# Where operand tiles begin inside 64 bytes: token tiles at a multiple of 64, weight tiles 32 bytes past one

## The chip, the cores and the metric

The kernel runs on one core of one Trainium2 chip. The metric is the device time of one execution in microseconds (us): the time before is 2825.68 us, the median of three runs from 2825.58 to 2825.96. A kernel's data lies in the core's on-chip memory (SBUF), 128 partitions wide; a tile's place is its first byte in every partition. TensorE multiplies: a stationary operand of up to 128 columns is loaded, and a moving operand of up to 512 columns streams past it.

## The reference, cut to what matters

Two blocks of two layers each work on 256 tokens of width 1024.

```
def reference(...):
    x = first_block(x, ...)      # 2 layers: x += mixers(rms(x) @ w_in) @ w_out
                                 #           x += peer_ffn(rms(x))
    return second_block(x, ...)  # 2 layers: x += merged(rms(x) @ w_in_2) @ w_o_2
                                 #           x += cross_attention(rms(x), rms(mem))
                                 #           x += (silu(h @ w1) * (h @ w3)) @ w2

def peer_ffn(x, w_query, sub_keys, down, up):   # 8 heads, top 16 of 16384 experts
    a = einsum('thkd,td->thk', down[ib], xb)
    c = gb * gelu(a)
    return einsum('thk,thkd->td', c, up[ib])
```

The kernel computes the expert layer densely: the activations of all 16384 experts (down), times a gate that is zero for the experts not chosen, times all of up. So nearly all work of both blocks is matrix products of a weight matrix with 256 tokens.

## The kernel before

**Three passes.** The products are float32. Every operand is split into a high part, rounded to the type fp32r, and a low part, what is left, and each product is made of three fp32r passes: high x high, and the two mixed ones. A weight chunk lands by DMA in `ring` (SyncE issues it some turns ahead), ScalarE copies it rounded into a high tile (`w_hi`, `out_hi`, `down_hi`, `up_hi` and others), and VectorE subtracts that from the raw one and writes the low tile (`ring_lo`, which lies over `ring`; `out_lo`, `down_lo`, `up_lo`). The token side has its own pairs: `h_t_hi` and `h_t_lo`, `h_t_expert` (the high part that goes with `h_t_lo` in the expert layer), `lead_x`, `held`, `coef`, `mt`, `ff`, `branch` and `ya`.

**Two shapes.** Where the result is wanted by channels, the weight tile is stationary (128 columns) and all 256 tokens are the moving operand: `channels` (L2648), `act_in_parts` (L1537), `passes_quarter` (L1480) and half of the front (L598). Where it is wanted by tokens, 128 tokens are stationary and 512 weight columns move: `tokens` (L2666), `branch` (L2925), `out_sums` (L1547), the held blocks (L1525) and the other half of the front (L607). In a row of the profile "ps<-a,b" is a product into PSUM with a moving and b stationary.

**Order.** Each engine has its list of instructions, written out by hand; semaphores order them across engines. TensorE runs one product after another, and the stationary operand of the next is loaded while the moving one of the present streams. In the peer loop 48 products of L1537 (one block of experts, 256 columns) alternate with 24 of L1547 (512 columns). The first 32 blocks of a layer's experts are held and summed by L1525 in one run of 768 products.

**Places.** Tiles are laid out one behind the other in the order of the code, `sb(...)` for those that stay; a `with ...: pass` gives its room back at once, so that the next tile lies over it. `arena` holds most of the rest, cut by `carve`, and tiles made by `over(...)` lie inside it. The first tile begins at byte 4224, a multiple of 64, and all sizes ahead of `hybrid_params` are multiples of 64 too. Its 69 numbers end 20 bytes past one; the next tile is put at the next multiple of 32. So before the change

- at a multiple of 64: `h_t`, `h_t_lo`, `ring` and `ring_lo`, `h_t_expert`;
- 32 bytes past one: everything behind, which is `out_hi`, `out_lo`, `coef`, `ya_hi`, `held`, `lead_x`, `first_hi`, `gate_hi`, `down`, `up`, `h_t_hi`, and in the second block `w_hi`, `mt`, `ff` and `branch`.

The pieces of these tiles that an instruction takes begin at multiples of 512 bytes within the tile, so that each operand has its tile's place inside 64 bytes.

Of the kernel before, what the change touches and what calls it, by code (L numbers as in the profile page):

```python
# [11 lines left out]
F32 = mybir.dt.float32  # L12
F32R = mybir.dt.float32r
# [4 lines left out]
P = 128  # L18
T = 256
D = 1024  # L20
TT = T // P
KD = D // P
# [22 lines left out]
GROUP = 8  # L45
# [5 lines left out]
STAGES = 4  # L51
GATES = T * NKEYS // 2
HELD = BLOCKS // 2
REACH = [(0, 0, 1, 16), (16, 1, 3, 8), (40, 4, 4, 4), (56, 8, 8, 1)]
REACHED = 64
PROB_BANKS = (4, 5, 6, 7, 2)
LEAD = HELD // 2 - 2
GATE_SPLIT = [LEAD, LEAD + 1]
# [4 lines left out]
for _n, _b in enumerate(LEAD_LOADS[4:]):  # L63
    LEAD_PLACE[_b] = LEAD_PLACE[_n]
LEAD_PLACE.update((b, ((0, 0), (1, 0), (0, 1))[b % 3]) for b in range(len(LEAD_LOADS), HELD))
LEAD_PLACE.update((b, (b % 2, 0)) for b in range(HELD, HELD + 2))
LOADS = LEAD_LOADS + list(range(len(LEAD_LOADS), HELD + 2))
LEAD_SLOTS = 5
FIRST_TURN = GATE_SPLIT[-1] + 1
OWN_X = FIRST_TURN + 2  # L70
TURNS = 2 * (HELD - FIRST_TURN)
TURN_HIGH = [next(s for s in range(GROUPS_OF_TOKENS) if QUARTER[s] >= 4 * (FIRST_TURN - LEAD) - 5 + 2 * n) for n in range(TURNS)]
# [25 lines left out]
HI_SLOTS, RAW_SLOTS, CHUNK_SIZE = 4, 8, 1024  # L98
# [80 lines left out]
N_SPAR = -(-N_SECOND // 16) * 16  # L179
N_Z3 = -(-2 * (T + 2) // 16) * 16  # L180
# [152 lines left out]
def build(nc, dram, out, steps):  # L333
    ctx = ExitStack()
    with ctx:
        def sb(name, shape, dt=F32):
            return ctx.enter_context(nc.sbuf_tensor(name, shape, dt))
# [9 lines left out]
        with nc.sbuf_tensor("h_t", [P, KD, T], F32) as HT:  # L347
            pass
        HT_LO = sb("h_t_lo", [P, KD, T], F32R)
        with nc.sbuf_tensor("ring_lo", [P, RAW_SLOTS, CHUNK_SIZE], F32R) as RAW_LO:  # L350
            pass
        RING = sb("ring", [P, 2, 4096])
        RAW = RING[:, :, :].rearrange("p a (b n) -> p (a b) n", n=CHUNK_SIZE)
        COMMON = sb("common_sb", [P, N_COMMON])
        with nc.sbuf_tensor("h_t_expert", [P, KD, T], F32R) as HT_EXPERT:
            pass
        PHASE = sb("phase_sb", [P, max(N_PHASE_CONST, KD * T)])
# [9 lines left out]
            pass  # L367

        with ExitStack() as second:
            second.enter_context(nc.sbuf_tensor("before_ya", [P, 3 * 512], F32))  # L370
            YA_HI = second.enter_context(nc.sbuf_tensor("ya_hi", [P, 2, T], F32R))
        GELU = sb("gelu", [P, 2, 512])
        COEF_HI, COEF_LO = sb("coef_hi", [P, 2, 512], F32R), sb("coef_lo", [P, 2, 512], F32R)
        KEYS = sb("keys", [P, P])
        with nc.sbuf_tensor("out_lo", [P, OUT_SLOTS, D], F32R) as OUT_LO:
            pass
        with nc.sbuf_tensor("hot_second1", [P, 2, GROUP, P], F16) as HOT2_ODD:
# [4 lines left out]
            pass  # L382
        sb("parts_room", [P, 4 * T])
        HOT2 = (HOT2_EVEN, HOT2_ODD)
        with nc.sbuf_tensor("arena", [P, 32768 + STAGES * GROUP * 64], F32) as ARENA:
            pass

        with ExitStack() as second:
            def over(name, shape, dt=F32R):
                return second.enter_context(nc.sbuf_tensor(name, shape, dt))  # L390

            BRANCH_LO = over("branch_lo", [P, KD, T])
            over("before_mem", [P, N_SPAR], F32)
            MT_HI, MT_LO = over("mt_hi", [P, KD, T]), over("mt_lo", [P, KD, T])
            over("before_w", [P, 2 * KD * T], F32)
            W_HI = over("w_hi", [P, HI_SLOTS, CHUNK_SIZE])
            FF_HI, FF_LO = over("ff_hi", [P, KF, T]), over("ff_lo", [P, KF, T])
            over("before_branch", [P, 4112], F32)
            BRANCH_HI = over("branch_hi", [P, 6, T])
        sb("arena_gates", [P, GATES])  # L400
        with nc.sbuf_tensor("held_lo", [P, HELD, 512], F32R) as HELD_LO:
            pass
        with nc.sbuf_tensor("before_gate_hi", [P, 17 * 512], F32), nc.sbuf_tensor("gate_hi0", [P, D], F32R) as GATE_HI0, \
                nc.sbuf_tensor("lead_x_hi", [P, KD, T], F32R) as LEAD_X_HI, nc.sbuf_tensor("lead_x_lo", [P, KD, T], F32R) as LEAD_X_LO, \
                nc.sbuf_tensor("first_hi", [P, 2, D], F32R) as FIRST_HI:
            pass
        DOWN_HI, DOWN_LO = sb("down_hi", [P, 2, 2 * D], F32R), sb("down_lo", [P, 2, 2 * D], F32R)
        UP_HI, UP_LO = sb("up_hi", [P, 2, 2 * D], F32R), sb("up_lo", [P, 2, 2 * D], F32R)
        with nc.sbuf_tensor("held_hi", [P, HELD_SLOTS, 512], F32R) as HELD_HI:
            pass  # L410
        with nc.sbuf_tensor("gate_hi1", [P, D], F32R) as GATE_HI1, nc.sbuf_tensor("gate_hi2", [P, D], F32R) as GATE_HI2:
            pass
        HT_HI = sb("h_t_hi", [P, KD, T], F32R)
        NUMBERS = sb("numbers", [P, P], F16)
# [68 lines left out]
        for n in (8, 8, 4, 2, 2):  # L483
# [9 lines left out]
        G = split(ARENA[:, 0:GATES], "p (t n) -> p t n", t=T)  # L493

        (SPAR, _, MT, MK, MV, _, Z3, YA, QKVG, ZG, GT, MER, QKR, QKT2, DM, MEMW), _ = carve(
            after_scr, N_SPAR, KD * T, KD * T, KD * T, TT * D, HI_SLOTS * CHUNK_SIZE, N_Z3, 2 * T, TT * 1536,
            TT * 512, TT * 3 * D, TT * D, TT * 512, 4 * T, 4 * (T + P), DEPTH * KD)
        FINAL = ARENA[:, after_scr + N_SPAR:after_scr + N_SPAR + D]
        WSM, VN, YC = (ONE[:, n * 512:(n + 1) * 512] for n in range(3))
# [208 lines left out]

        def late_stage(n):

            return 32768 + (n % STAGES if n >= STAGES else n - STAGES) * GROUP * 64

        def gates_of(n):

# [2728 lines left out]
```

## Time and profile before

| | |
|---|---|
| time of three runs, median | 2825.68 us |
| profiled execution: its own time | 2825.48 us |
| profiled execution: span of the core | 2823.7 us |
| granted TensorE clock, mean | 0.999 |
| TensorE matmuls busy | 2803.2 us, 99% of the span, 18566 of them |
| TensorE weight loads busy (beside them) | 2528.1 us, 90% |
| VectorE, ScalarE, GpSimd busy | 1943.8, 1419.7, 148.4 us |
| moved by DMA | 530.21 MB, 188 GB/s |

Busy is the time in which at least one instruction of the engine is under way. The span goes from the first instruction to the last; the execution's own time has 1.8 us around it. Matmuls overlap each other, so that the duration of one is longer than the time from its start to that of the next. "L2666" is line 2666 of the kernel.

### The profile page before, as it was taken

How to read it: one execution, taken by the hardware profiler on the slowest of the kernel's cores; microseconds unless marked ns; L12 is line 12 of the kernel's file. 1: busy time of each engine (PE TensorE's matmuls, PEld its weight loads, DVE VectorE, ACT ScalarE, POOL GpSimd, SP SyncE). 2: the span in 40 equal slices, each digit the busy share in tenths (PEclk: the TensorE clock that was granted, in tenths of full speed). 3: DMA queues.
4: the chain of work that ended last, by engine and by line, in shares of the span. 5: the costliest groups of instructions: out<-in, count | busy, mean ns of one | idle time of the engine just before them, and what ended most of it. 6: DMA issues, size and time to landing. Idle time of an engine off the chain costs nothing.

```text
span 2823.7 us, 45734 instructions
## 1 busy us (share of the span) xinstructions
PE 2803.2 (99%) x18566; PEld 2528.1 (90%) x18566; DVE 1943.8 (69%) x2882; ACT 1419.7 (50%) x1707; POOL 148.4 (5%) x145
## 2 busy tenths in 40 slices
PE   8999999999999999999999999999999999999998
PEld 7899998899999889999889999988899988888997
DVE  7889888655555788988865555576656556565664
ACT  6653554544444665355454444455455444545543
POOL 0033110000000003311000000000000000000000
PEclk9999999999999999999999999999999999999999
DMA  6344666855553534466685555465555656554663
GB/s 214 124 162 138 218 247 208 287 213 199 186 194 141 187 120 158 141 217 239 205 288 215 194 192 193 149 223 170 181 166 182 187 188 185 171 180 155 175 187 133
DMA packets 219570, 530.21 MB, mean 188 GB/s; under 512 B 13546, under 2 KB 87440, under 8 KB 208400
## 3 DMA queue, kind: packets, MB, share of 16 engines
q1 hardware_dynamic: 212944, 504.32, 54.2%
q0 software_dynamic: 6464, 23.61, 2.1%
q8 instruction: 116, 1.90, 0.3%
q14 instruction: 46, 0.38, 0.1%
HBM read 507.81 MB, written 20.06 MB: 187 GB/s over the span
## 4 chain that ended last, share of the span: by engine, by line
PE 98%; DVE 1%; DMA 1%; issue 0%; ACT 0%; SPq 0%; DVEq 0%
PE ps L2666 17%; PE ps L2648 13%; PE ps L1537 13%; PE ps L1547 12%; PE ps L1525 12%; PE ps L1480 11%; PE ps L607 4%; PE ps L598 4%; PE ps L1451 2%; PE ps L2925 2%; PE ps L1462 1%; PE ps L1255 1%; PE ps L2834 0%; PE ps L2818 0%; DMA ring<-in_peer_down 0%; PE ps L1367 0%
## 5 line engine op out<-in xcount | busy, mean ns | idle before, releaser
L2267 DVE TENSOR_TENSOR ring_lo<-ring,w_hi 128x1024 fp32r<-128x1024 f32 x320 | 388.2, 1224 | 243.0 <-ACT w_hi L2263 241.7
L2263 ACT ACTIVATE w_hi<-ring 128x1024 fp32r<-128x1024 f32 x320 | 335.2, 1056 | 236.1 <-PE ps L2666 169.0
L1537 PE MATMUL ps<-h_t_lo,down_hi 128*128 128x256 f32 x1024 | 288.2, 281 | 0.0
L1537 PE MATMUL ps<-h_t_expert,down_lo 128*128 128x256 f32 x1024 | 287.8, 281 | 0.0
L1537 PE MATMUL ps<-h_t_expert,down_hi 128*128 128x256 f32 x1024 | 286.8, 280 | 0.0
L2648 PE MATMUL ps<-h_t_lo,w_hi 128*128 128x256 f32 x928 | 260.7, 281 | 0.0
L2648 PE MATMUL ps<-h_t_hi,w_hi 128*128 128x256 f32 x928 | 259.4, 280 | 0.1
L2648 PE MATMUL ps<-h_t_hi,ring_lo 128*128 128x256 f32 x928 | 259.0, 279 | 0.0
L1143 ACT ACTIVATE out_hi<-ring 128x1024 fp32r<-128x1024 f32 x128 | 135.7, 1060 | 162.0 <-PE ps L1525 154.6
L2030 DVE TENSOR_TENSOR up_lo<-ring,up_hi 128x2048 fp32r<-128x2048 f32 x64 | 146.7, 2292 | 97.7 <-ACT up_hi L1134 97.7
L2023 DVE TENSOR_TENSOR out_lo<-ring,out_hi 128x1024 fp32r<-128x1024 f32 x128 | 156.6, 1224 | 77.1 <-ACT out_hi L1143 77.1
L1547 PE MATMUL ps<-up_hi,coef_hi 128*128 128x512 f32 x512 | 200.6, 392 | 0.0
L1547 PE MATMUL ps<-up_hi,coef_lo 128*128 128x512 f32 x512 | 199.9, 390 | 0.0
L1547 PE MATMUL ps<-up_lo,coef_hi 128*128 128x512 f32 x512 | 199.4, 390 | 0.0
L1525 PE MATMUL ps<-out_hi,held_hi 128*128 128x512 f32 x512 | 199.4, 389 | 0.0
L1525 PE MATMUL ps<-out_hi,held_lo 128*128 128x512 f32 x512 | 199.2, 389 | 0.0
L1525 PE MATMUL ps<-out_lo,held_hi 128*128 128x512 f32 x512 | 199.2, 389 | 0.0
L1134 ACT ACTIVATE up_hi<-ring 128x2048 fp32r<-128x2048 f32 x64 | 122.7, 1917 | 150.5 <-PE ps L1547 147.2
L1537 PEld LDWEIGHTS ps<-h_t_lo,down_hi 128*128 128x128 f32 x1024 | 193.0, 188 | 2.4
L1537 PEld LDWEIGHTS ps<-h_t_expert,down_hi 128*128 128x128 f32 x1024 | 192.5, 188 | 2.4
L1537 PEld LDWEIGHTS ps<-h_t_expert,down_lo 128*128 128x128 f32 x1024 | 193.3, 189 | 0.0
L2666 PE MATMUL ps<-w_hi,h_t_hi 128*128 128x512 f32 x448 | 180.3, 403 | 0.4 <-DVE ring_lo L2267 0.4
(532 smaller groups left out, 7403.5 us busy)
## 6 DMA issues: line engine op xcount, KB each, us to landing
ring<-in_peer_down SPq DMA_DIRECT2D x128, 1024.0 KB, 5.6
ring<-in_w_in SPq DMA_DIRECT2D x140, 512.0 KB, 3.7
ring<-in_peer_up SPq DMA_DIRECT2D x66, 1024.0 KB, 4.8
ring<-in_w SPq DMA_DIRECT2D x132, 512.0 KB, 3.8
ring<-in_peer_up SPq DMA_DIRECT2D x124, 512.0 KB, 4.2
late_gates<-arena POOLq DMA_DIRECT2D x64, 256.0 KB, 5.2
arena<-late_gates SPq DMA_DIRECT2D x16, 1024.0 KB, 6.4
ring<-in_w_out SPq DMA_DIRECT2D x16, 512.0 KB, 4.1
```

The source lines that it names most:

```text
L1134: a.e.activation(to[:, slot, :], raw(which, slot), ACT.Copy).then_inc(*a.count(name))
L1143: a.e.activation(OUT_HI[:, out_slot(b, j), :], up_raw(b, j), ACT.Copy).then_inc(*a.count(f"up_hi{b}{j}"))
L1480: m = pe.e.matmul(PS[:, act_bank(b), j * T:(j + 1) * T], w[:, o], x[:, kc, :], start=kc == 0 and n == 0, stop=kc == KD - 1 and n == 2)
L1525: m = pe.e.matmul(PS[:, 2 * t + half, :], x, w, start=b == 0 and j == 0 and n == 0, stop=False, skip_group_check=True)
L1537: m = pe.e.matmul(PS[:, 4 + b, j * T:(j + 1) * T], w[:, b, o], x[:, kc, :], start=kc == 0 and n == 0, stop=kc == KD - 1 and n == 2)
L1547: m = pe.e.matmul(PS[:, 2 * t + half, :], x[:, b, c], w[:, b, o], start=False, stop=last and n == 2, skip_group_check=True)
L2023: v.e.tensor_tensor(OUT_LO[:, out_slot(b, j), :], up_raw(b, j), OUT_HI[:, out_slot(b, j), :].bitcast(F32), ALU.subtract) \
L2030: v.e.tensor_tensor(lo[:, slot, :], raw(which, slot), hi[:, slot, :].bitcast(F32), ALU.subtract) \
L2263: a.e.activation(W_HI[:, g % HI_SLOTS, :], RAW[:, g % RAW_SLOTS, :], ACT.Copy).then_inc(*a.count(f"c{g}_hi"))
L2267: v.e.tensor_tensor(RAW_LO[:, g % RAW_SLOTS, :], RAW[:, g % RAW_SLOTS, :], W_HI[:, g % HI_SLOTS, :].bitcast(F32), ALU.subtract).then_inc(* ...
L2648: m = pe.e.matmul(PS[:, bank, c * T:(c + 1) * T], w[:, kc, c * P:(c + 1) * P], y[:, 4 * n + kc, :], start=n == 0 and c == 0 and kc == 0 an ...
L2666: m = pe.e.matmul(PS[:, bank + t, :], y[:, k0 + kc, o], w[:, kc, :], start=first and kc == 0 and i == 0, stop=last and kc == 1 and i == 2)
```

## The change

Unused tiles of 32 bytes (8 numbers of float32 in each partition) are put between others, so that afterwards every token-side operand tile begins at a multiple of 64 bytes and every weight-side one 32 bytes past one. `ring_lo` and `ring` go from 0 to 32; `h_t_hi`, `lead_x`, `held`, `coef`, `ya_hi`, `mt`, `ff` and `branch` go from 32 to 0; `h_t_lo` and `h_t_expert` stay at 0, and `out`, `down`, `up`, `w_hi`, `first_hi` and `gate_hi` at 32. Where room inside `arena` had to be kept for it, offsets move with it (`LATE_AT`, the size of one piece of `carve`), and `gate_hi1` and `gate_hi2` now stand ahead of `held_hi`. No instruction changes but for its addresses.

```diff
+LATE_AT = GATES + 512 * HELD + 16
...
         HT_LO = sb("h_t_lo", [P, KD, T], F32R)
+        sb("before_ring", [P, 8])
         with nc.sbuf_tensor("ring_lo", [P, RAW_SLOTS, CHUNK_SIZE], F32R) as RAW_LO:
             pass
         RING = sb("ring", [P, 2, 4096])
         RAW = RING[:, :, :].rearrange("p a (b n) -> p (a b) n", n=CHUNK_SIZE)
         COMMON = sb("common_sb", [P, N_COMMON])
+        sb("before_phase", [P, 8])
         with nc.sbuf_tensor("h_t_expert", [P, KD, T], F32R) as HT_EXPERT:
             pass
...
-            second.enter_context(nc.sbuf_tensor("before_ya", [P, 3 * 512], F32))
+            second.enter_context(nc.sbuf_tensor("before_ya", [P, 3 * 512 + 8], F32))
             YA_HI = second.enter_context(nc.sbuf_tensor("ya_hi", [P, 2, T], F32R))
         GELU = sb("gelu", [P, 2, 512])
+        sb("before_coef", [P, 8])
         COEF_HI, COEF_LO = sb("coef_hi", [P, 2, 512], F32R), sb("coef_lo", [P, 2, 512], F32R)
         KEYS = sb("keys", [P, P])
+        sb("behind_keys", [P, 8])
...
-        with nc.sbuf_tensor("arena", [P, 32768 + STAGES * GROUP * 64], F32) as ARENA:
+        sb("before_arena", [P, 8])
+        with nc.sbuf_tensor("arena", [P, LATE_AT + STAGES * GROUP * 64], F32) as ARENA:
             pass
...
-            over("before_w", [P, 2 * KD * T], F32)
+            over("before_w", [P, 2 * KD * T + 8], F32)
             W_HI = over("w_hi", [P, HI_SLOTS, CHUNK_SIZE])
+            over("behind_w", [P, 8], F32)
             FF_HI, FF_LO = over("ff_hi", [P, KF, T]), over("ff_lo", [P, KF, T])
...
-        with nc.sbuf_tensor("before_gate_hi", [P, 17 * 512], F32), nc.sbuf_tensor("gate_hi0", [P, D], F32R) as GATE_HI0, \
+        with nc.sbuf_tensor("before_gate_hi", [P, 17 * 512 + 8], F32), nc.sbuf_tensor("gate_hi0", [P, D], F32R) as GATE_HI0, \
+                nc.sbuf_tensor("before_lead_x", [P, 8], F32), \
...
+                nc.sbuf_tensor("before_first", [P, 8], F32), nc.sbuf_tensor("first_hi", [P, 2, D], F32R) as FIRST_HI:
             pass
+        sb("before_down", [P, 8])
         DOWN_HI, DOWN_LO = sb("down_hi", [P, 2, 2 * D], F32R), sb("down_lo", [P, 2, 2 * D], F32R)
         UP_HI, UP_LO = sb("up_hi", [P, 2, 2 * D], F32R), sb("up_lo", [P, 2, 2 * D], F32R)
+        with nc.sbuf_tensor("gate_hi1", [P, D], F32R) as GATE_HI1, nc.sbuf_tensor("gate_hi2", [P, D], F32R) as GATE_HI2:
+            pass
+        sb("before_h_t_hi", [P, 8])
         with nc.sbuf_tensor("held_hi", [P, HELD_SLOTS, 512], F32R) as HELD_HI:
...
-            after_scr, N_SPAR, KD * T, KD * T, KD * T, TT * D, HI_SLOTS * CHUNK_SIZE, N_Z3, 2 * T, TT * 1536,
+            after_scr, N_SPAR, KD * T, KD * T, KD * T, TT * D, HI_SLOTS * CHUNK_SIZE + 16, N_Z3, 2 * T, TT * 1536,
...
-            return 32768 + (n % STAGES if n >= STAGES else n - STAGES) * GROUP * 64
+            return LATE_AT + (n % STAGES if n >= STAGES else n - STAGES) * GROUP * 64
```

## Rows read from the trace of the kernel before

**Rows 1.** The page, busy us (share of the span) and instructions of each engine.
```profile
PE 2803.2 (99%) x18566; PEld 2528.1 (90%) x18566; DVE 1943.8 (69%) x2882; ACT 1419.7 (50%) x1707; POOL 148.4 (5%) x145
```

**Rows 2.** TensorE's waits: us in total, times, longest.
```profile
PE ps L763 <- DMA common_sb<-in_common: 7.2, 1, 7.2
PE ps L1480 <- DVE ring_lo L668: 2.3, 2, 1.8
...
PE ps L2666 <- DVE ring_lo L2267: 0.4, 1, 0.4
```

**Rows 3.** The page, the chain that ended last, by engine.
```profile
PE 98%; DVE 1%; DMA 1%; issue 0%; ACT 0%; SPq 0%; DVEq 0%
```

**Rows 4.** Groups of matmuls by line: shapes, count | busy us, mean ns | idle.
```profile
L1537 PE MATMUL ps<-h_t_lo,down_hi 128*128 128x256 f32 x1024 | 288.2, 281 | 0.0
L2648 PE MATMUL ps<-h_t_lo,w_hi 128*128 128x256 f32 x928 | 260.7, 281 | 0.0
...
L1525 PE MATMUL ps<-out_hi,held_hi 128*128 128x512 f32 x512 | 199.4, 389 | 0.0
L2666 PE MATMUL ps<-w_hi,h_t_hi 128*128 128x512 f32 x448 | 180.3, 403 | 0.4 <-DVE ring_lo L2267 0.4
...
L2666 PE MATMUL ps<-w_hi,ff_hi 128*128 128x512 f32 x176 | 69.9, 397 | 0.0
...
L607 PE MATMUL ps<-ring_lo,h_t_hi 128*128 128x512 f32 x160 | 62.9, 393 | 0.0
...
L2666 PE MATMUL ps<-w_hi,mt_hi 128*128 128x512 f32 x64 | 26.7, 417 | 0.0
...
L2925 PE MATMUL ps<-w_hi,branch_lo 128*128 128x512 f32 x64 | 25.1, 393 | 0.0
```

**Rows 5.** Stretch 1700 to 1848 us: busy us of each engine, granted clock, DMA share, GB/s.
```profile
1700.00:1848.00 148.00, 148.00 (x952) 134.93 (x951) 81.31 (x54) 62.17 (x54) 0.00 (x0) 1.00 0.46 163
```

**Rows 6.** The chain in order of time: start us, length us, what, count of matmuls.
```profile
97.60 5.50 PE ps L607 x24
...
138.86 13.98 PE ps L607 x60
...
184.86 23.05 PE ps L1480 x192
...
233.15 17.14 PE ps L1480 x144
...
403.54 174.15 PE ps L1525 x768
...
1887.25 22.20 PE ps L2666 x96
...
1995.58 19.42 PE ps L2925 x84
...
2159.03 127.20 PE ps L2648 x1080
...
2286.23 61.32 PE ps L2666 x264
...
2377.59 32.96 PE ps L2666 x144
```

**Rows 7.** The same chain from 1497 to 1560 us, the peer loop.
```profile
1520.11 5.47 PE ps L1547 x24
1525.58 5.67 PE ps L1537 x48
...
1547.88 5.68 PE ps L1537 x48
```

**Rows 8.** The same chain from 2098 to 2160 us.
```profile
2116.03 1.73 PE ps L2834 x8
```

**Rows 9.** The page, DMA issues: count, KB each, median us to landing.
```profile
ring<-in_w SPq DMA_DIRECT2D x132, 512.0 KB, 3.8
```

More of the change, by code:

```diff
@@ L402, in build @@
             pass
-        with nc.sbuf_tensor("before_gate_hi", [P, 17 * 512], F32), nc.sbuf_tensor("gate_hi0", [P, D], F32R) as GATE_HI0, \
+        with nc.sbuf_tensor("before_gate_hi", [P, 17 * 512 + 8], F32), nc.sbuf_tensor("gate_hi0", [P, D], F32R) as GATE_HI0, \
+                nc.sbuf_tensor("before_lead_x", [P, 8], F32), \
                 nc.sbuf_tensor("lead_x_hi", [P, KD, T], F32R) as LEAD_X_HI, nc.sbuf_tensor("lead_x_lo", [P, KD, T], F32R) as LEAD_X_LO, \
-                nc.sbuf_tensor("first_hi", [P, 2, D], F32R) as FIRST_HI:
+                \
+                nc.sbuf_tensor("before_first", [P, 8], F32), nc.sbuf_tensor("first_hi", [P, 2, D], F32R) as FIRST_HI:
             pass
+        sb("before_down", [P, 8])
         DOWN_HI, DOWN_LO = sb("down_hi", [P, 2, 2 * D], F32R), sb("down_lo", [P, 2, 2 * D], F32R)
         UP_HI, UP_LO = sb("up_hi", [P, 2, 2 * D], F32R), sb("up_lo", [P, 2, 2 * D], F32R)
+        with nc.sbuf_tensor("gate_hi1", [P, D], F32R) as GATE_HI1, nc.sbuf_tensor("gate_hi2", [P, D], F32R) as GATE_HI2:
+            pass
+        sb("before_h_t_hi", [P, 8])
         with nc.sbuf_tensor("held_hi", [P, HELD_SLOTS, 512], F32R) as HELD_HI:
-            pass
-        with nc.sbuf_tensor("gate_hi1", [P, D], F32R) as GATE_HI1, nc.sbuf_tensor("gate_hi2", [P, D], F32R) as GATE_HI2:
             pass
```

## The prediction

> **What bounds the kernel now.** I read the busy table first, then TensorE's waits, then the chain that ended last. TensorE's matmuls are busy for 2803.2 of 2823.7 us, 99% [rows 1]. In the whole span it waits for another engine or a transfer in six places, 11.6 us together (7.2 for the first load, then 2.3, twice 0.6, 0.5 and 0.4) [rows 2]. The chain is TensorE for 98% [rows 3]. So only one number can move much: how soon a matmul starts behind the one before it. The printed duration of a matmul does not give that, because matmuls overlap: it is 281 ns for 256 columns and 389 ns for 512 [rows 4]. The chain in order of time does: a piece of one line lasts as long as its matmuls follow each other, and its length over its count is the pitch.
>
> Pitches from it, at a granted clock of 1.00 (the 2.4 GHz level) [rows 5]:
> - 512 columns, moving and stationary tile both 32 past a multiple of 64 ("at 32"): L1525 174.15 / 768 = 226.8 ns; L1547 5.47 / 24 = 227.9 ns [rows 6, 7].
> - 512 columns, moving tile alternating between at 32 and at 0 (w_hi or out, then ring_lo): L2666 with h_t 22.20 / 96 = 231.3 and 32.96 / 144 = 228.9 ns; L2666 with ff 61.32 / 264 = 232.3; L2925 19.42 / 84 = 231.2; L607 13.98 / 60 = 233.0 and, in a short piece, 5.50 / 24 = 229.2 [rows 6].
> - 256 columns, token tile (moving) at 0, weight tile (stationary) at 32, as everywhere after the change: L1537 5.67 / 48 = 118.1, and 5.68 in other turns: 118.2 ns [rows 7].
> - 256 columns, mixed places: L2648 127.20 / 1080 = 117.8; L1480, nearly all at 32, 17.14 / 144 = 119.0 to 23.05 / 192 = 120.1 [rows 6].
> - For scale, a plain float32 product of 256 columns (L2834), which streams them at half rate: 1.73 / 8 = 216.3 ns [rows 8]. That is what 512 full-rate columns would take if nothing held the stream up, so L1525 loses 10.5 ns a matmul, L2666 up to 16.
>
> Two things speak for the addresses as the cause of these differences. L1525 and L2666 have the same shape, type and clock, and differ in tiles alone. Within L2666 the ff pieces are slower than the h_t pieces, and there too only the tile changes. Against it: two h_t pieces of one line have 231.3 and 228.9, so the place is not all; how the streams were in step when the piece began must count too.
>
> **The change, part by part.**
> No instruction is added, removed or moved in any queue. The unused tiles are never touched. What changes is the first byte of nearly every tile, by 0 to some hundred bytes.
>
> (a) 512 columns with alternating moving tiles. Counts from the groups: L2666 448 x 3 with h_t, 176 x 3 with ff, 64 x 3 with mt; L2925 192 (two passes of 64 with w_hi, one with ring_lo, the tiles of branch and ya together); L607 480 (160 with ring_lo, so 3 x 160) [rows 4]; together 2,736. After it the moving tile is at 32 in every pass, as in L1525, and the stationary one at 0. Present pitch, weighted: 1,344 at 230.5 (between the two h_t pieces), 720 (ff, mt) at 232.3, 192 at 231.2, 480 at 230.5 (between L607's two): 231.0 ns. If a steady moving place is what gives L1525 its 226.8, the gain is 2,736 x 4.2 = 11.5 us. Ends: 0 (pitch stays 231.0), or worse up to 233.3 (the L607 piece's 233.0, rounded up), and 224 ns, an estimate one step of 3 ns beyond L1525, as far as L2666's two h_t pieces lie apart.
>
> (b) L1525, 512 x 3 [rows 4], and L1547, of the same number,, are already steady in the moving tile. Their stationary tiles (coef, held) go from 32 to 0: from "same place" to "opposite place". No 512-column row of before has a moving tile at 32 and its next stationary tile at 0, so this price is open on both sides. The nearest rows are 256 columns wide: L1537 with opposite places has 118.2, L2648, where the tile being loaded and the one streaming mostly share a place, 117.8, and L1480 with nearly all at 32 has 119.0 to 120.1. The three lie on both sides of each other, so I take nothing: 0 us. Ends: they rise to today's alternating pitch of 231.0, 1,536 x 4.2 + 1,536 x 3.1 = +11.2 us; or they fall to 224, 1,536 x 2.8 + 1,536 x 3.9 = -10.3 us.
>
> (c) 256 columns. L1537's 3,072 matmuls keep their arrangement: 0. L2648 (928 x 3 with h_t [rows 4], and 128 x 3 with mt: 3,168) goes to it, 117.8 to 118.2: +1.3 us. In L1480 about 1,440 matmuls stream lead_x, now at 32; 119.3 to 118.2: -1.6 us. L598, some 1,000 with places as mixed as L2648's, is left at nothing. Together -0.3 us; ends -3 and +5.
>
> (d) The other engines. VectorE is busy 1943.8 us of the span [rows 1], ScalarE less; if a float32 pass of theirs over a shifted tile cost some per cent more, the slack between loads and use covers it, as the waits of TensorE on VectorE inside the stream are 4.4 us in total [rows 2]. From 1700 to 1848 us TensorE does not stop at all and the transfers take 46% of the engines [rows 5]. If that cover went, the first thing late would be L1480's ring_lo, 2.3 us today [rows 2]. The ring's own address moves with "before_ring" from a multiple of 64 to 32 past one, so transfers land at another offset; 512 KB take 3.8 us to land and are issued some turns ahead [rows 9]. I cost (d) at 0, with +3 us as its bad end. A faster TensorE takes the buffers up sooner by 0.4%, which this slack also covers.
>
> Sum: 0 - 11.5 + 0 - 0.3 + 0 = -11.8 us. The profiled execution took 2825.5 us by its own time (2823.7 of span), 0.2 under the median of the runs shown. 2825.5 - 11.8 = 2813.7, say 2814.
>
> The Trainium skill speaks against any of this. "SBUF — State Buffer", in "SBUF: two separate sides", has TensorE on ports of its own, waiting on no one, and "TensorE: Matmul & The Clock Gate", in "What happens when you issue a matmul", gives the moving and the stationary operand a read port each. By these the place of a tile would cost nothing, and the time would be that of rival 2. The second page's "Back-to-back issue gap" (columns over the clock and 2.5 ns) would give 109.2 and 215.8 ns; only the half-rate row, 216.3, agrees with it, and the pitches of L1537 and L1525 stand 9 and 11 ns above. Something that these pages don't have holds full-rate float32 streams up.
>
> **The rivals.**
> 1. Opposite places are the bad arrangement at 512 columns (slower). The moving stream and the load of the next stationary tile run side by side behind each other's start. At present L1525 sits at its lowest pitch for hundreds of matmuls with both at 32; shifting one of them by half the 64 bytes puts it out of that step. Then all 5,808 matmuls of 512 columns go at 231.0: +11.2 us from (b), nothing from (a), -0.3 from (c): 2836.4. At 233.3 throughout it is 5,808 x 2.3 = 13.4 us more, 2850. It decides as soon as L1525 and L1547 lose more than (a) gains: above about 229.1 ns for all of them. For it: L1525, the best row, has same places, and L2925 and the ff pieces, whose loads in the ring_lo pass are from the opposite place, are slower than the h_t pieces, where that load is from the same one. Against it: L1537 with opposite places is not worse than L1480 with same ones.
> 2. Nothing to see. Either the tile's place matters only through how the streams happened to fall into step, or (a) and (b) meet half way: all 512-column matmuls at 229 ns give 2,736 x -2.0 + 1,536 x 2.2 + 1,536 x 1.1 = -0.4 us: 2825. For it: one line with two pitches. Against it: L1525's 768 matmuls in a row at 226.8 [rows 6], which no alternating piece reaches.
> 3. Opposite places are better than anything seen at 512 columns: 224 ns for all 5,808. 2,736 x 7.0 + 1,536 x 2.8 + 1,536 x 3.9 = 29.4 us: 2796. The hard end, no hold-up at all (216.3), would be 2,736 x 14.7 + 1,536 x 10.5 + 1,536 x 11.6 = 74 us; I leave it out, because L1537 has opposite places already and still stands at 118.2 against half of 216.3.
>
> **How the numbers follow.** Forecast (steady moving place wins, stationary place indifferent): 0.36, its own range 2808 to 2819. Rival 3: 0.09. Rival 2: 0.22. Rival 1: 0.33. Faster or slower is told here by 0.2%, 5.65 us, so below 2820.0 or above 2831.3: faster 0.36 + 0.09 = 0.45, the same 0.22, slower 0.33. The predicted time is the likeliest case's, 2814. The range has to take in most of rival 1 and part of rival 3: 2800 to 2842; outside are the far halves of those two, about 0.17.
>
> **What would show it.** In the chain in order of time: L2666's piece of 264 at 59.9 us instead of 61.32, and that of 96 at 21.8 instead of 22.2 (step a); L1525's 768 at 174.2 us and L1547's 24 at 5.47 (step b: 177.4 and 5.54 are rival 1, 172.0 and 5.38 rival 3); L2648's 1080 at 127.6 and L1537's 48 still at 5.67 (step c); TensorE's waits still about 11 us (step d). The prediction is wrong if L1525's piece changes by more than 1.5 us either way, or if L2666's does not fall.

## The result, and the profile after

The kernel with the change takes 2852.01 us (median of 4 runs, 2849.85 to 2853.5) against 2825.63: 1.0093 times as long, interval 1.0075 to 1.011. The forecast was 2814 with a range of 2800 to 2842, so it missed on the wrong side. The profiled execution took 2853.5 us, 28.0 more than that of before. Of the executions of the experiments below one, of e11_tokens_16, ran at a granted clock of 0.653 and took 3963.48 us; it is left out of that run's ratio.

The page after, busy us of each engine, and TensorE's waits (us in total, times, longest); they answer to [rows 1, 2]:
```profile
PE 2832.3 (99%) x18566; PEld 2536.8 (89%) x18566; DVE 1944.4 (68%) x2882; ACT 1420.7 (50%) x1707; POOL 149.8 (5%) x145
```
```profile
PE ps L774 <- DMA common_sb<-in_common: 6.8, 1, 6.8
PE ps L1491 <- DVE ring_lo L679: 2.1, 2, 1.8
...
PE ps L2677 <- DVE ring_lo L2278: 0.2, 1, 0.2
```
Counts are the same, VectorE and ScalarE are as busy as before, and TensorE waits 10.4 us instead of 11.6. So the loss lies in how soon one matmul starts behind another. A line after has its number of before plus 11 (L1525 is L1536, L1537 L1548, L1547 L1558, L1480 L1491, L2648 L2659, L2666 L2677, L2925 L2936, L598 L609, L607 L618).

The chain in order of time (start, length, what, count), answering to [rows 6, 7]:
```profile
141.30 14.23 PE ps L618 x60
...
187.73 22.95 PE ps L1491 x192
...
235.93 17.20 PE ps L1491 x144
...
406.14 179.22 PE ps L1536 x768
...
596.67 5.59 PE ps L1558 x24
602.27 5.67 PE ps L1548 x48
...
1909.36 22.39 PE ps L2677 x96
...
2018.69 19.63 PE ps L2936 x84
...
2182.97 127.98 PE ps L2659 x1080
2310.95 61.60 PE ps L2677 x264
...
2402.73 33.59 PE ps L2677 x144
```
Length over count: L1536 233.4 ns (226.8 before), L1558 232.9 (227.9), L2677 with h_t 233.2 and 233.3 (231.3 and 228.9), with ff 233.3 (232.3), L2936 233.7 (231.2), L2659 118.5 (117.8), L1548 118.1 as before. L618's piece of 60 gives 237.2, but its first start-to-start distance is 314 ns and the other 59 average 233.0 (229.0 before, behind a first one of 306). So the lines of 512 columns now stand at 233 to 234, where before they lay between 226.7 and 232.3.

The distance from each matmul's start to the next in the two traces, summed by line (worked out from the start times, and called the summed starts below), gives the account: L1536 +9.9 us, L1558 +7.8, L2677 +3.4, L618 +2.9, L2659 +2.2, L1491 and L609 +1.9 together, L1462 +0.8, L2936 +0.4, L1548 -0.7; with the rest +28.4. Of L618's 2.9, 1.1 are in its 480 products of 512 columns, the rest in 192 of 256.

### The profile page after: what moved, and what is told of

Its sections match the earlier page's. It is cut to its first block, busy times and chain, and to the rows that moved or that the text cites. A ratio compares the mean times of both kernels' runs of the same rounds, so it can differ in the third digit from the quotient of the medians.

```text
span 2851.7 us, 45734 instructions
## 1 busy us (share of the span) xinstructions
PE 2832.3 (99%) x18566; PEld 2536.8 (89%) x18566; DVE 1944.4 (68%) x2882; ACT 1420.7 (50%) x1707; POOL 149.8 (5%) x145
## 4 chain that ended last, share of the span: by engine, by line
PE 98%; DVE 1%; DMA 1%; issue 0%; ACT 0%; SPq 0%; DVEq 0%
PE ps L2677 17%; PE ps L2659 13%; PE ps L1548 13%; PE ps L1536 13%; PE ps L1558 13%; PE ps L1491 11%; PE ps L618 4%; PE ps L609 4%; PE ps L1462 2%; PE ps L2936 2%; PE ps L1473 1%; PE ps L1266 1%; PE ps L2845 0%; PE ps L2829 0%; DMA ring<-in_peer_down 0%; PE ps L1378 0%
## 5 line engine op out<-in xcount | busy, mean ns | idle before, releaser
L1548 PE MATMUL ps<-h_t_lo,down_hi 128*128 128x256 f32 x1024 | 287.9, 281 | 0.0
L1548 PE MATMUL ps<-h_t_expert,down_hi 128*128 128x256 f32 x1024 | 286.8, 280 | 0.0
L1548 PE MATMUL ps<-h_t_expert,down_lo 128*128 128x256 f32 x1024 | 286.2, 279 | 0.0
L2659 PE MATMUL ps<-h_t_hi,w_hi 128*128 128x256 f32 x928 | 262.0, 282 | 0.1
L2659 PE MATMUL ps<-h_t_hi,ring_lo 128*128 128x256 f32 x928 | 261.2, 281 | 0.0
L2659 PE MATMUL ps<-h_t_lo,w_hi 128*128 128x256 f32 x928 | 259.8, 280 | 0.0
L1558 PE MATMUL ps<-up_lo,coef_hi 128*128 128x512 f32 x512 | 204.2, 399 | 0.0
L1536 PE MATMUL ps<-out_hi,held_lo 128*128 128x512 f32 x512 | 203.2, 397 | 0.0
L1536 PE MATMUL ps<-out_hi,held_hi 128*128 128x512 f32 x512 | 202.8, 396 | 0.0
L1558 PE MATMUL ps<-up_hi,coef_hi 128*128 128x512 f32 x512 | 202.0, 395 | 0.0
L1536 PE MATMUL ps<-out_lo,held_hi 128*128 128x512 f32 x512 | 201.2, 393 | 0.0
L1558 PE MATMUL ps<-up_hi,coef_lo 128*128 128x512 f32 x512 | 200.6, 392 | 0.0
L1548 PEld LDWEIGHTS ps<-h_t_expert,down_hi 128*128 128x128 f32 x1024 | 195.1, 191 | 3.0
L1548 PEld LDWEIGHTS ps<-h_t_lo,down_hi 128*128 128x128 f32 x1024 | 191.5, 187 | 2.6
L1548 PEld LDWEIGHTS ps<-h_t_expert,down_lo 128*128 128x128 f32 x1024 | 193.5, 189 | 0.0
L2677 PE MATMUL ps<-w_hi,h_t_hi 128*128 128x512 f32 x448 | 180.6, 403 | 0.2 <-DVE ring_lo L2278 0.2
```

Source lines behind the costliest of these rows:

```text
L1536: m = pe.e.matmul(PS[:, 2 * t + half, :], x, w, start=b == 0 and j == 0 and n == 0, stop=False, skip_group_check=True)
L1548: m = pe.e.matmul(PS[:, 4 + b, j * T:(j + 1) * T], w[:, b, o], x[:, kc, :], start=kc == 0 and n == 0, stop=kc == KD - 1 and n == 2)
L1558: m = pe.e.matmul(PS[:, 2 * t + half, :], x[:, b, c], w[:, b, o], start=False, stop=last and n == 2, skip_group_check=True)
L2659: m = pe.e.matmul(PS[:, bank, c * T:(c + 1) * T], w[:, kc, c * P:(c + 1) * P], y[:, 4 * n + kc, :], start=n == 0 and c == 0 and kc == 0 an ...
L2677: m = pe.e.matmul(PS[:, bank + t, :], y[:, k0 + kc, o], w[:, kc, :], start=first and kc == 0 and i == 0, stop=last and kc == 1 and i == 2)
```

## The rule that the experiments led to

In cycles of the 2.4 GHz level (the mean granted clock is 0.998 to 1.0 in every profiled execution), 226.7 ns are 544 cycles and 233.3 ns 560. Three passes, from a start to the third start behind it, are 1632 or 1680 in a steady stream, and every sum that repeats exactly from turn to turn (816, 848, 864, 1632, 1648, 1664, 1680) is a multiple of 16 cycles, 6.67 ns. What mostly decides between 544 and 560 is how far the stationary tile begins behind the moving one, modulo 256 bytes: their distance. The places modulo 256, from the order and sizes of the tiles:

| | before | after |
|---|---|---|
| held_hi, held_lo | 32, 32 | 0, 192 |
| out_hi, out_lo | 32, 32 | 96, 160 |
| coef; up | 32; 32 | 128; 224 |
| down; h_t_expert | 32; 192 | 224; 0 |
| h_t_hi, h_t_lo | 32, 128 | 0, 128 |
| w_hi, ring_lo; ff | 224, 128; 224 | 160, 160; 192 |

The change moved tiles by different sums of 32-byte steps. L1525 and L1547 had stationary and moving tile at distance 0 before; after it their distances are 96 and 160. L2677's are 96 and 224 with h_t and 32 with ff. The map of the next section has 560 to 562.6 cycles at each of these.

The map tells the pitch of a stream that keeps one distance. Where distances alternate it need not: L2666 with h_t had 64, 160 and 160 in turn before, 560 cycles each in the map, and its three passes repeat at 1664 cycles in the piece of 96 and at 1648 in that of 144, with the same tiles at the same places.

## Experiments

**A map of distances (e5_map).** 60 equal products a line, one stationary tile and one moving tile of 512 columns; only the line's stationary place differs:
```
sta_032x = tile("sta_032x", 128, 32)      # begins 32 bytes past a multiple of 512
for i in range(60): last = eng.matmul(PS[:, 2, 0:512], sta_032x, mov_a[:, 0:512], start=i == 0, stop=i == 59)
```
Before it came a smaller table of pairs (e1_pairs), planned by the rule modulo 64. Both leave out the whole reference computation, and in both no other engine runs an instruction while TensorE multiplies.

> A kernel that only loads x, rounds it into ten small fp32r tiles, and then has TensorE do 60 products in a row for each pair of a moving tile (at 0, 16, 32 or 64 bytes inside 128) and a stationary one (at 0, 16, 32, 48, 64 or 96), first with 512 columns, then with 256; it leaves out the whole reference computation, and writes x out. Theory (only the distance between the two places inside 64 bytes counts, opposite is bad at 512 columns): 226.7 ns a product where both are equal modulo 64 (0/0, 0/64, 32/32, 32/96, 64/0, 64/64), 233.3 where they are 32 apart; the 16s in between. Rival A (a stationary tile at a multiple of 64 is bad wherever the moving one is): 0/0, 64/0, 64/64 at 233.3 too, 0/32 at 226.7. Rival M (the place plays no part in a steady run; only a change of tile between passes costs): one value for all pairs. At 256 columns all theories expect 117.5 to 119 ns for every pair.

> As e1_pairs (the reference computation is left out, x is written out), but the distance between the two tiles is laid out over 512 bytes: one moving tile at 0 with 32 stationary tiles 16 bytes apart, one moving tile at 32 with 16 stationary tiles 32 bytes apart, 60 products each, with 512 and with 256 columns. e2 to e4 threw out the rule of equal places modulo 64: with all tiles at a multiple of 64 the ff products stayed at 232.2 ns, and with coef and up both at 32 modulo 64 they stayed at 233.3. In all runs so far 226.7 ns goes with both tiles at one place modulo 512. Theory D (the distance modulo 512 counts): 226.7 ns at distance 0, above 229 at most others, 233.3 at 96 and 128; the second moving tile shows the same values at the same distances. Rival A (own places count): the two moving tiles differ at equal distance. Rival H (only how the streams happened to fall into step counts): no pattern by distance. At 256 columns theory D expects 113.3 ns at distance 64, as in e1_pairs for one pair, and 117.5 to 120 elsewhere.

The small table took 523.34 us. It had no pair under 549.3 cycles at 512 columns and values from 549.3 to 562, which places modulo 64 did not sort. By their distances modulo 256, worked out afterwards, none of its pairs has 0, 16 or 240, and with the moving tile at a multiple of 32 its values at 512 columns are the map's within 3 cycles (549.3 at 192, 560 at 160, 562.5 at 96). In the map the lines L86, L87, ... have the stationary tile 0, 16, 32, ... bytes past the moving one. The chain in order of time:
```profile
29.06 13.61 PE ps L87 x60
42.67 13.99 PE ps L88 x60
...
126.62 14.00 PE ps L94 x60
...
182.41 13.74 PE ps L98 x60
...
224.15 13.62 PE ps L101 x60
237.77 13.60 PE ps L102 x60
...
264.98 13.99 PE ps L104 x60
...
682.77 7.19 PE ps L134 x60
...
711.22 6.81 PE ps L138 x60
...
774.96 7.00 PE ps L147 x60
781.96 7.00 PE ps L148 x60
```
At 512 columns only distances 16 (L87), 240 (L101) and 0 (L102 is 256, the same modulo 256) have 13.60 to 13.62 / 60 = 226.7 to 227.0 ns; 32 (L88) and 128 (L94) have 233.3, 192 (L98) 229.0. From 256 on the values of 0 to 255 come again (L104 as L88), and with the moving tile at 32 instead of 0 they go by distance as well. At 512 columns all of them agree within 3 cycles. At 256 columns some distances have two values: 64 has 282.7 cycles there and 272.0 here, 224 has 280.0 and 282.7 behind that one moving tile, and in e1_pairs 128 and 144 once have 288.0 where the map has 284.7 and 284.0. At 256 columns distance 0 (L134) is among the worst, 7.19 / 60 = 119.8; 208 and 224 (L147, L148) have 116.7, and 64 (L138) 113.5. So 512 and 256 columns want different distances.

**All tiles at 0 modulo 64 (e2_all_at_0).** The kernel before with one more tile:
```
+        sb("behind_stat", [P, 8])
```


> The kernel before with one unused tile of 32 bytes behind stat, so that every operand tile, token and weight, begins at a multiple of 64. Theory (equal places are good at 512 columns): all 5,808 products of 512 columns at 226.7 ns: against before 2,736 x 4.3 + 1,536 x 1.2 = 13.6 us less, and 256 columns within 3 us of before: 2811 to 2815 us, ratio 0.995 to 0.996. Rival A (a stationary tile at a multiple of 64 is bad): 512 columns at 233.3 as after the change, 2850 us. Rival M (only the alternation of the moving tile's place costs, as the prediction had it): also about 2812, so this run tells theory and M from A, and not from each other.

2821.82 us (2820.89 to 2824.14), ratio 0.9986, interval 0.9977 to 0.9996.
```profile
402.93 174.15 PE ps L1526 x768
...
2281.09 61.02 PE ps L2667 x264
```
The expected 2811 to 2815 did not come. The alternating line is still at 61.02 / 264 = 231.1 ns (232.3 before), though all its tiles are at 0 modulo 64. Steadiness modulo 64 is not what it lacks. By the distances modulo 256 nothing in L1526 and L1548 has changed (both tiles at 64), and they keep their pitch: 226.8 ns in the first piece, and 1632 cycles for three passes of L1548. The 4 us gained are, in the summed starts, -3.4 in L1538, -2.1 in L1548 (fewer slow starts at the head of its pieces), -1.6 in L1481 and +2.4 in L2649.

**Parts of the change (e3_coef_held_back, e4_ring_only).** The first is the kernel after with coef, held_hi and held_lo back at 32 modulo 64; the second the kernel before with only the ring moved modulo 64. Modulo 256 e4 moves more: the ring goes from 128 to 160, and every tile behind phase_sb 64 bytes on, coef, held, out, up, w and ff together. The lines are some of several:
```
-        sb("before_coef", [P, 8])             # e3, from the kernel after
...
+        sb("before_ring", [P, 8])             # e4, from the kernel before
+        sb("before_phase", [P, 8])            # e4
```


> The changed kernel with coef, held_hi and held_lo alone put back to 32 bytes past a multiple of 64; all others as changed. Theory: L1536 and L1558 go from 233.3 back to 226.7 (768 products in 174.1 us, 24 in 5.44 to 5.47), 3,072 x 6.6 = 20 us less than after the change: 2832 us, the rest stays slow (L2677 264 in 61.6). Rival A says the same. Rival M (steady moving tile is good): nothing changes here, about 2852.

> The kernel before with ring and ring_lo alone moved to 32 past a multiple of 64, so that the moving tile of every 512-column product is at 32 in all three passes while the stationary tiles stay where they were (h_t_hi, ff, mt, branch at 32; h_t_lo at 0). This is step (a) of the prediction alone. Theory (equal places): products with ff, mt and branch go from 232 to 226.7 ns (912 x 5.4 = 4.9 us); those with h_t_hi, h_t_lo have one load of three opposite and stay between 227 and 233; L1525 and L1547 stay at 226.8 and 227.9; 2816 to 2821 us. Rival M: 2,736 x 4.2 = 11.5 us less, 2814. Rival A: h_t_lo at 0 is bad in one of three, about the same as the theory.

e3: 2849.65 us (2848.43 to 2852.98), 1.0083 (1.0066 to 1.0099). It should have given back 20 us, and gave back 2, within the scatter of both kernels' executions (4.6 between the two traces, 1.5 of it in L618, where no place changed). Coef is then at 96, up at 224: distance 128, and L1558 stays at 5.60 / 24 = 233.3. L1536 has a mixture of distances (128 and 64) and falls to 177.52 / 768 = 231.1.

e4: 2832.64 us (2831.16 to 2836.5), 1.0022 (1.0013 to 1.0032).
```profile
2162.93 126.85 PE ps L2650 x1080
2289.78 61.59 PE ps L2668 x264
...
2381.72 33.61 PE ps L2668 x144
```
With the ring at 32 every moving tile of 512 columns has one place modulo 64, which step (a) was to gain 11.5 us with. The run is 7 slower: L2668 goes to 233.3 and 233.4 ns in both pieces. L1527, whose two tiles moved together and keep distance 0, stays at 174.16 us for its 768. The summed starts give +2.9 us in L2668, +2.0 in L2650, +1.3 in the 512-column products of L609.

**The deciding run: one tile by 128 bytes (e13_coef_128).** The kernel before, with coef alone moved; 128 is a multiple of 64, and all other tiles keep their place modulo 256:
```
+        sb("before_coef", [P, 32])
         COEF_HI, COEF_LO = ...
+        sb("behind_coef", [P, 32])
```


> The kernel before, with the coef tiles alone 128 bytes further (and 128 unused bytes behind them, so that every other tile keeps its place modulo 256). By the prediction's rule (place modulo 64) nothing changes: 128 is a multiple of 64, 2826 us, L1549's three passes in the trace at 1632 cycles of 2.4 GHz as before. By theory D (distance modulo 256) the stationary coef tile and the moving up tile now stand 128 apart, which the map has at 560 cycles (233.3 ns): three passes at 1680 instead of 1642 on average (1632 with some slow starts), 1536 products x 5.4 ns = 8.3 us: 2834 us, everything else as before.

2834.91 us (2833.67 to 2836.09), 1.0032 (1.002 to 1.0045).
```profile
1525.12 5.59 PE ps L1549 x24
1530.71 5.67 PE ps L1539 x48
...
2168.18 127.20 PE ps L2650 x1080
2295.38 61.32 PE ps L2668 x264
```
Of these pieces only the coef line's moved, from 5.47 [rows 7] to 5.59; L2650 and L2668 have to the last digit the 127.20 and 61.32 of before [rows 6]. In the summed starts that line has +7.8 us, the same +7.8 as in the kernel after; the rest of the 9.2 is L600's 0.8 and crumbs.

**All tiles at one place modulo 256 (e6_one_place).** Distance 0 for every product:
```
-N_SPAR = -(-N_SECOND // 16) * 16
+N_SPAR = -(-N_SECOND // 64) * 64
-N_Z3 = -(-2 * (T + 2) // 16) * 16
+N_Z3 = -(-2 * (T + 2) // 64) * 64
+        sb("before_phase", [P, 48])
+        sb("behind_stat", [P, 40])
-            over("before_branch", [P, 4112], F32)
+            over("before_branch", [P, 4160], F32)
```


> The kernel before with every operand tile at one place modulo 256 bytes (128 past a multiple), by unused room and two sizes rounded up. Theory D (in a steady run the distance between the stationary and the moving tile modulo 256 sets the pitch; e5_map): distance 0 everywhere, so all 5,808 products of 512 columns at 226.7 ns, L2666's ff pieces included (264 in 59.9 us, which equal places modulo 64 did not do in e2), and all of 256 columns at 120.0 ns (288 cycles), slower than before: 512 columns -13.6 us, 256 columns + 3,072 x 1.8 + 3,168 x 2.2 + 2,784 x 1.3 + 1,008 x 2 = +18 us: about 2830 us. Rival H (only the step into which the streams fall by their start): 512 columns keep a mixture as in e2, 2820 to 2826 us.

2832.44 us (2830.88 to 2835.14), 1.0021 (1.0012 to 1.003).
```profile
405.65 174.11 PE ps L1527 x768
...
1520.56 5.75 PE ps L1539 x48
1526.31 5.47 PE ps L1549 x24
...
2165.68 129.60 PE ps L2650 x1080
2295.28 59.87 PE ps L2668 x264
...
2385.68 32.67 PE ps L2668 x144
```
The alternating line, at 229 to 232 ns before, is at 226.8 and 226.9: the 59.9 us for the piece of 264 that the prediction wanted to see, reached by another rule. The same distance is bad at 256 columns: L2650 120.0 ns, L1539 119.8. The summed starts: -8.1 us in L2668, +6.8 in L2650, +5.1 in L1539, +2.3 in L1482, +2.2 in L600.

**Weights 16 bytes past the tokens (e7_16_apart).** The distances are 16 and 240, which the map had at 544 cycles for 512 columns and about 284 for one of the two at 256. The weight tiles are slices that begin 16 bytes into a larger one:
```
+        RAW_LO = past16(RAW_LO_, RAW_SLOTS, CHUNK_SIZE)      # tile[:, 4:4 + n]; ring, out, w_hi, first, gate, down, up alike
```


> All token tiles at 128 modulo 256, all weight tiles at 144, 16 bytes further. Theory D by e5_map: 512 columns (weight moving, token stationary, distance -16) 226.7 ns; 256 columns (token moving, weight stationary, distance +16) 118.2 ns. 5,808 at 226.7 is -13.6 us against before, 256 columns within 2 us of before: about 2813 us, the best of both shapes at once. Rival H: between 2818 and 2826 us.

2845.34 us (2844.34 to 2847.16), 1.0065 (1.0051 to 1.0078): a clear miss.
```profile
1523.85 5.56 PE ps L1569 x24
1529.41 5.68 PE ps L1559 x48
...
2306.97 61.16 PE ps L2688 x264
```
At 256 columns it came as forecast (118.3). At 512 it is 231.7 instead of 226.7. All moving tiles of the map had begun at a multiple of 32; here they don't.

**A second map (e9_map16).** Moving tile 16 past a multiple of 32, and three passes in turn:
```
for i in range(60): last = mm(3, 512, (sta_000x, sta_000x, sta_000y)[i % 3], (mov_at_16[:, 0:512], mov_at_16_2[:, 0:512], mov_at_16[:, 0:512])[i % 3], i, 60)
```


> A small kernel of matmuls alone (its output is its input, copied; nothing of the reference is computed): 60 products a line. First a moving tile that itself begins 16 bytes past a multiple of 32, with the stationary tile at each multiple of 16 from 0 to 240, at 512 and at 256 columns. Then three passes in turn as in the big kernel (two moving tiles and two stationary tiles, each pair at one place) at 512 columns: moving 0 / stationary 0, 0 / 240, 0 / 16, 16 / 0, 16 / 16; and at 256 columns with moving 0: stationary 0, 224, 208, 64, 16, 240, 208, 224, 0, 64, 0, 16, so that a place comes up behind different predecessors. Theory D (distance modulo 256 alone): the map of the first moving tile repeats, moved by 16: 544 cycles of 2.4 GHz (226.7 ns) at distances 0, 16 and 240, 560 (233.3 ns) at most others, also for 16 / 0 in three passes. Theory M (the moving tile must also begin at a multiple of 32): with the moving tile at 16, distance 240 (moving 16, stationary 0) is about 556 cycles (231.7 ns) as the run with the weights 16 past had, in one pass and in three; moving 0 / stationary 240 and 0 / 16 in three passes stay at 544. Theory E (the entry decides): the 256-column lines differ between their first and second appearance, by up to 10 cycles (4 ns).

Worked out from the starts 21 to 57 of each line, in cycles:

| moving at, distance | 512 columns | 256 columns |
|---|---|---|
| 16, 0 | 560.0 | 284.0 |
| 16, 16 | 544.0 | 280.9 |
| 16, 32 | 544.0 | 288.0 |
| 16, 112 | 560.0 | 272.0 |
| 16, 224 | 557.3 | 284.0 |
| 16, 240 | 556.0 | 280.0 |
| 16, in three passes: 0 / 240 | 554.7 / 556.0 | |
| 0, in three passes: 0 / 16 / 240 | 544.0 / 544.0 / 544.0 | 288.0 / 283.7 / 288.0 |
| 0, in three passes: 64, first and second time | | 272.0, 282.7 |
| 0, in three passes: 208 and 224, both times | | 280.0 |

Theory M holds: the distance decides only together with the moving tile's own place modulo 32, and 16 at distance 240 has 556.0, which is e7's 231.7 ns. Theory E holds for one distance of this map: 64 had 272.0 cycles the first time and 282.7 the second, with nothing else changed but what ran ahead of it. The others came out alike both times.

**Moving the tiles that only 256 columns use (e8_down_64, e10_256_off_32).** e6 with the down tiles 64 bytes further; then instead 224 further, with lead_x 32 further (distance 224 both):
```
+        sb("before_down", [P, 16])            # e8;   [P, 56] in e10
         DOWN_HI, DOWN_LO = ...
+        sb("behind_down", [P, 48])            # e8;   [P, 8] in e10
+                nc.sbuf_tensor("before_lead_x", [P, 8], F32), \        # e10
```


> e6_one_place with the two down tiles alone 64 bytes further than the rest, so that L1537 has distance 64, which in e5_map and e1_pairs gave 113.3 ns a product of 256 columns behind one moving tile and 117.8 behind the other. Theory D with the locked step: L1537's 48 in 5.44 us, 3,072 x 6.7 = 20.6 us less than e6, about 2809 us. If the low pitch is a matter of how the run is entered: 5.65 us, 6.8 us less than e6, about 2823 us.

> All tiles at one place modulo 256 as in the run that had 2832, except the two that only products of 256 columns use: the down tiles 32 bytes earlier than a multiple of 256 from their moving tiles (distance 224), and lead_x 32 bytes later than its stationary tiles (distance 224 too). In the map a distance of 224 had 280.0 cycles (116.7 ns) against 288.0 (120.0 ns) at distance 0. Theory D: the down line's three passes go from 864 to 840 cycles, 3072 products x 3.3 ns = -10.2 us, lead_x 1440 x 3.3 = -4.8 us: 2832.4 - 15.0 = 2817 us, the fastest of all so far. Theory E (the entry decides, as with down at distance 64, which the map had at 272 and the kernel at 282.7): 282.7 to 284 cycles there, 2832.4 - 4500 x 1.9 ns = 2824 us.

e8: 2827.06 us (2824.71 to 2827.68), 0.9999 (0.9989 to 1.0008); down's three passes went from 864 to 848 cycles, the 282.7 of the map's second line and not its 272. e10: 2820.77 us (2818.67 to 2822.46), 0.9979 (0.997 to 0.9988).
```profile
1130.46 11.20 PE ps L1486 x96
...
1148.57 16.96 PE ps L1486 x144
...
1523.94 5.60 PE ps L1543 x48
1529.54 5.47 PE ps L1553 x24
```
L1543 is at 116.7 ns as the map had it, and L1486 at 116.7 and 117.8 (the three passes of lead_x at 842.2 cycles on average, 840 by the map). Against e6 the down line has -9.9 us in the summed starts (-10.2 expected) and L1486 -2.8 (-4.8). This is a version below both kernels, by 0.2% under before and 1.1% under after.

**Tokens 16 bytes past the weights (e11_tokens_16, e12_tokens_16_down_128).** From the second map: moving weights at a multiple of 32 with the stationary token 16 further (544), and moving tokens at 16 with distance 240 (280):
```
+        HT, HT_LO = past16(HT_), past16(sb("h_t_lo", [P, KD * T + 8], F32R))     # h_t_hi, h_t_expert, lead_x alike
...
+        sb("before_down", [P, 32])            # e12 only
...
```


> All tiles at one place modulo 256 as in the run that had 2832, but h_t, h_t_lo, h_t_hi, h_t_expert and lead_x (the token tiles that stream at 256 columns and are loaded at 512) begin 16 bytes further. By the two maps: at 512 columns the moving tile is a weight at a multiple of 32 and the stationary one 16 further, 544 cycles of 2.4 GHz (226.7 ns) as at distance 0; at 256 columns the moving tile is at 16 past a multiple of 32 and the stationary one 16 earlier (distance 240), 280.0 cycles (116.7 ns) instead of 288.0. Theory M (distance and the moving tile's own place modulo 32 decide): 9600 products of 256 columns (2784 + 3072 + 2784 + 960) x 3.33 ns = -32 us, 512 columns unchanged: 2832.4 - 32 = 2800 us. Rival E (in three passes in turn the moving place 16 has another cycle, 284, as most of its row has): -16 us, 2816. Rival: the 512-column products lose their 544 as in the run with the weights 16 past (231.7 ns, 2064 + 480 products): +12, 2812.

> The same with the down tiles 128 bytes further, so that their distance from the moving h_t tiles is 112; the map with the moving tile 16 past a multiple of 32 had 272.0 cycles (113.3 ns) there, its lowest value. Theory M: 3072 products x 3.33 ns = -10 us more, 2790 us. Rival E (the entry decides, as at distance 64, which had 272.0 and 282.7 in one kernel, behind different predecessors): between 280 and 284, 2800 to 2805.

e11: 2820.9 us (median of all eleven executions), 0.9978 (0.9969 to 0.9988). e12: 2820.18 us (2813.55 to 2823.08), 0.9978 (0.9967 to 0.9988). Both missed their 2800 and 2790. The 512-column lines mostly kept their 226.7 (L1532, ff and about half of the h_t products of L2673; the other half are at 233.3, at the same distance of 16), but the 256-column ones did not take 280: 854.4 cycles for three passes in the down line, 848.2 in L2655 with h_t. Three passes at 256 columns with the moving tile 16 past had not been mapped. In e12 the down line, for which the run was made, did not take its 816 but 854.8. A warning lay in the first table: at distance 112 with the moving tile 16 past, e1_pairs had 284.7 cycles, and the 272.0 came from e9 alone. Another line got faster instead. L1487 in e11 and L1489 in e12 are the same products, here with tiles whose byte addresses are the same in both:
```profile
304.21 2.86 PE ps L1487 x24
...
307.98 2.90 PE ps L1487 x24
```
```profile
306.48 2.78 PE ps L1489 x24
...
310.17 2.78 PE ps L1489 x24
```
In e12 its steady three passes are 816 cycles (113.3 ns a product), in e11 852; that line alone is 7.7 us shorter. Of e12's 8 runs two took 2813.6 and 2814.5, one of them the profiled one, and six 2820 to 2823. That those six missed the 816 is likely but argued only: they have no profile. What made the difference at equal addresses no run shows.

## Why the prediction was wrong, point by point

- **What bounds the kernel** was right: TensorE's pitch, and nothing else. Step (d) held, with 10.4 us of waits against 11.6 and no transfer late.
- **Step (a)** failed, in its mechanism. It read L2666's alternation of places modulo 64 as the cause of its slower pitch and wanted a steady moving place. e2 made everything steady modulo 64 and left the ff piece at 61.02 us; e4 gave the moving tiles one place modulo 64, and lost 7 us in all; and after the change w_hi and ring_lo share one place even modulo 256 (160), at 233.3 ns. What separates L2666 from L1525 in [rows 6] is that its tiles stood 64 and 160 apart modulo 256 with h_t, 0 and 96 in turn with ff, and L1525's 0 throughout; e6 brought them to 0 and had 59.87. The steadiness was a coincidence of the one good row. Forecast -11.5 for 2,736 products; measured +4.9 (L2677 3.4, L2936 0.4, L618 1.1).
- **Step (b)** was the larger miss: forecast 0, range -10.3 to +11.2, measured 9.9 + 7.8 = +17.7 us. The bad end was priced with the mean of the alternating lines (231.0). The one row above it that the prediction had, 233.0 in L607 [rows 6], is no pitch: the piece holds one distance of 306 ns, and the other 59 average 229.0. So no row showed 233.3, and the size of this loss could not be read from them. e13 shows the mechanism with coef alone.
- **Step (c)** stayed between its ends of -3 and +5, with the wrong sign: L2659 +2.2 (+1.3 forecast), L1548 -0.7 (0), L1491 +0.4 (-1.6), L609 +1.5 (0), together +3.4 against -0.3. That it stayed small is likely the mean of many distances, which no run separates; e6 shows that distance 0 throughout costs 16 us against before in these four lines.
- **Rival 1** was nearest: opposite places bad, "at 233.3 throughout it is 2850". Its price a product was right and its reason was not, since e13 keeps both tiles at 32 modulo 64 and still has the 233.3. That its total came within 2 us of the measured time is in part luck: the 5,808 products lost 22.6 us where it had 24.6, and the other 5.8 us, nearly all from products of 256 columns and f16, it did not price. It was given 0.33, and the range cut off its far end, the one that came.
- **The period.** The rows could not tell modulo 64 from modulo 256: L1525's tiles share a place in both. Nor could the two h_t pieces with 231.3 and 228.9 ns: they have the same tiles, so no rule on places alone separates them (they lie 2.4 ns apart, not the 3 that the 224 was built on). The prediction took its period, 64 bytes, from the words of the change; no row gave it.

The page "SBUF — State Buffer" of the Trainium skill, section "SBUF: two separate sides", has TensorE on ports of its own, waiting on no other engine. Nothing here contradicts that: in the map no other engine runs beside TensorE, and 233.3 ns came all the same. But the prediction took from it that places cost nothing, which is rival 2, and there the measured +26 us decide against it: the pitch goes with the places of TensorE's own two operands.

## What to carry to other kernels

Where TensorE is bound by full-rate float32 products, compute each pair's distance (stationary minus moving tile, modulo 256 bytes) before moving anything: a kernel that stands at distance 0 for its 512-column products (226.7 ns) loses 3% of them by a shift that looks harmless, and tiles used at 256 columns alone want 208 or 224 (116.7 against 120.0 ns; 224 once had 117.8), all with the moving tile at a multiple of 32. A change of padding is seldom local: an unused tile moves what follows it, as in e4, so give it back behind the tile and change one pair at a time. A rule on addresses read from the rows of one kernel is best measured by itself first, over the whole period.

## What the runs showed of the hardware that was not expected

- The pitch of full-rate float32 products depends on addresses with a period of 256 bytes: 226.7 to 234.4 ns at 512 columns, 113.3 to 120.2 at 256. Plain float32 at half rate shows nothing of it (1.73 us for 8 products before and after, L2845), nor do the f16 products beyond 0.8 us of 56.
- Steady streams step by 16 cycles, 6.67 ns; means between are cycles that mix steps. What grid this is no run shows.
- At some places a stream has more than one steady cycle: at 256 columns 272.0 or 282.7 at distance 64, where only what ran ahead differed within one program, and 816 or 852 for three passes in the last two kernels; at 512 columns 1648 or 1664 in L2666, and 1632 or 1680 in e11's L2673. The times of e12 fall in two groups (2814 and 2821), which this may explain. How to enter the fast cycle on purpose stays open, and with it the 2790 to 2800 us that the map promised.
- With the moving tile 16 past a multiple of 32 the map is another one (560.0 cycles at distance 0 instead of 544.0). Distances for places 4 or 8 past one were not tried.
